# Half the tokens of a product-key expert layer taken from row gathers to dense products over all experts

## What is computed

```
q = (hc @ w_query).reshape(TOKEN_CHUNK, PEER_HEADS, 2, PEER_HALF)
s = einsum('thpd,pkd->thpk', q, sub_keys)
s1, i1 = top_k(s[:, :, 0], 16)
s2, i2 = top_k(s[:, :, 1], 16)
cand = s1[..., :, None] + s2[..., None, :]
top_s, top_c = top_k(cand, 16)
idx = e1 * 128 + e2
g = softmax(top_s)
u = expert_down[idx]
a = gelu(einsum('thkd,td->thk', u, hc))
return einsum('thk,thkd->td', g * a, expert_up[idx])
```

## Time and profile before

| what | value |
|---|---|
| median of three runs | 3043.16 us (3043.06, 3043.16, 3046.47) |
| span of the profiled execution | 3041.3 us |
| PE busy | 2310.2 us |
| DVE busy | 2213.0 us |
| ACT busy | 2033.8 us |
| POOL busy | 1290.5 us |
| moved by DMA | 1152.07 MB, 379 GB/s over the span |
| of it by the gathers' queue | 1075.90 MB |

### The profile page before, as it was taken

The page is one execution under the profiler, slowest core; times in us unless marked ns, Lnnn a source line. Parts: engine busy times, 40 slices in busy tenths (PEclk is TensorE's granted clock), DMA queues, the critical chain, the costliest instruction groups (busy, mean ns, idle before and its releaser), DMA issues.

```text
span 3041.3 us, 38261 instructions
## 1 busy us (share of the span) xinstructions
PE 2310.2 (76%) x13098; PEld 1887.2 (62%) x13098; DVE 2213.0 (73%) x5241; ACT 2033.8 (67%) x3757; POOL 1290.5 (42%) x1164
## 2 busy tenths in 40 slices
PE   8999889888878966777666676677777777666766
PEld 4765577776765656666656566566566666555655
DVE  7897678899965967777776666677776666777744
ACT  4234268898866756776676767766776677666665
POOL 1003144444434644454454444444444444454543
PEclk9999999999989977776677777777677777776766
DMA  6252499999999999999999999999999999999997
GB/s 232 32 209 79 163 382 417 405 401 418 413 415 403 398 419 421 420 421 421 419 419 420 417 415 415 421 415 422 420 408 419 419 417 411 419 417 421 419 421 329
DMA packets 174835, 1152.07 MB, mean 379 GB/s; under 512 B 23472, under 2 KB 25392, under 8 KB 43440
## 3 DMA queue, kind: packets, MB, share of 16 engines
q0 software_dynamic: 147984, 1075.90, 85.7%
q1 hardware_dynamic: 26656, 73.72, 6.6%
HBM read 1142.60 MB, written 5.77 MB: 378 GB/s over the span
## 4 chain that ended last, share of the span: by engine, by line
DMA 37%; DVE 21%; PE 16%; ACT 11%; issue 5%; POOL 1%; POOLq 0%; DVEq 0%; ACTq 0%
DMA pair<-in_experts_dram,idx_g 36%; DVE pair L1942 10%; PE acc_a L1563 5%; ACT pair L1719 5%; PE acc_b L1563 3%; PE pef L1538 2%; ACT w L1717 1%; ACT L1715 1%; PE acc_b L1486 1%; PE turns L1502 1%; POOL pair L1392 1%; ACT L1710 1%; ACT ga L1715 1%; DVE top_i L1870 1%; DVE staged L1871 1%
## 5 line engine op out<-in xcount | busy, mean ns | idle before, releaser
L1392 POOL DMA_INDIRECT pair<-in_experts_dram,idx_g x1024 | 1226.5, 1198 | 1431.3 <-PE acc_a L1563 803.1
L1942 DVE SCALAR_TENSOR_TENSOR pair<-pair,h 128x1024 f32<-128x1024 f32 x1024 | 1247.6, 1221 | 647.3 <-DMA pair<-in_experts_dram,idx_g 645.4
L1719 ACT ACTIVATE pair<-pair,w 128x1024 f32<-128x1024 f32 x1024 | 1176.4, 1149 | 33.3
L1563 PE MATMUL acc_a<-ident,pair 128*128 128x128 f32 x5120 | 853.1, 327 | 364.4 <-ACT pair L1719 361.0
L1563 PEld LDWEIGHTS acc_a<-ident,pair 128*128 128x128 f32 x5120 | 720.4, 170 | 488.7 <-ACT pair L1719 462.3
L1563 PE MATMUL acc_b<-ident,pair 128*128 128x128 f32 x3072 | 595.4, 362 | 288.2 <-ACT pair L1719 287.9
L1563 PEld LDWEIGHTS acc_b<-ident,pair 128*128 128x128 f32 x3072 | 489.9, 188 | 387.2 <-ACT pair L1719 381.6
L1715 ACT ACTIVATE ga<-a 128x1 f32<-128x1 f32 x1024 | 204.4, 200 | 652.5 <-DVE pair L1942 644.2
L1717 ACT ACTIVATE w<-ga,g 128x1 f32<-128x1 f32 x1024 | 301.7, 295 | 33.2
L1538 PE MATMUL pef<-h2t,wq 128*128 128x128 f32 x1536 | 198.7, 293 | 5.9 <-DMA wq<-in_w_query_t_dram 5.9
L1538 PEld LDWEIGHTS pef<-h2t,wq 128*128 128x128 f32 x1536 | 196.8, 211 | 6.2 <-issue 6.2
(11 more groups left out here) (378 smaller groups left out, 2273.3 us busy)
## 6 DMA issues: line engine op xcount, KB each, us to landing
pair<-in_experts_dram,idx_g POOLq DMA_INDIRECT x1024, 13.8
wrow<-in_w_ada_t_dram SPq DMA_DIRECT2D x12, 1024.0 KB, 6.0
pieces<-in_w_query_t_dram SPq DMA_DIRECT2D x18, 512.0 KB, 8.5
wada<-in_w_ada_t_dram SPq DMA_DIRECT2D x16, 512.0 KB, 9.7
wq<-in_w_query_t_dram SPq DMA_DIRECT2D x4, 2048.0 KB, 29.7
out_dram<-h SPq DMA_DIRECT2D x8, 512.0 KB, 8.3
wout_b<-in_w_out_dram SPq DMA_DIRECT2D x1, 4096.0 KB, 33.8
x<-in_x_dram SPq DMA_DIRECT2D x7, 512.0 KB, 12.9
```

Of the source, the lines that this page charges most:

```text
L1392: p.indirect_dma_start(pair[n % R], None, A["experts"], bass.IndirectOffsetOnAxis(ap=idx[:, t % (2 * PH), k:k + 1], axis=0)).then_inc(pair ...
L1563: last = t.matmul(accs[ACC[i]][:, k * P:(k + 1) * P], pair[n % R][:, D + k * P:D + (k + 1) * P], S.ident[:], is_transpose=True, start=n % ...
L1719: s_.activation(pair[n % R][:, D:], pair[n % R][:, D:], ACT.Copy, scale=w[:, n % NA:n % NA + 1]).then_inc(scaled, 1)
L1942: v.scalar_tensor_tensor(down, down, 1.0, h2[:, n // P, :], ALU.mult, ALU.mult, accum_out=a[:, n % NA:n % NA + 1]).then_inc(dotted, 1)
```

## The change

Tiles 0 to 3 keep the gathers, so that `SLOTS` is now 512. Tiles 4 to 7 (512 tokens) are computed over all 16384 experts: first product, gelu, a gate matrix that is zero for the experts a token has not chosen, second product. The experts are taken as 128 chunks of 128, chunk c holding the experts whose second index is c; two new inputs, `down_t` and `up_t`, hold the same weights in that order.

The parts, in the slots' order:

- The tasks 18 to 63 are asked in slots 257 to 302, one per slot, and found in slots 258 to 303, all six parts in one slot. For tiles 4 to 7 the find ends with the two indices and the gates as lists of 128 per token (`lists`) and makes no row index.
- In slots 283, 291, 299 and 307 PE turns a tile's three lists so that tokens lie along the free axis. The masks follow in sixteen slots of eight groups each (284, 285, 288, 289, 292, ... 312, 313). A group is four tokens: DVE makes for each a 128x128 matrix with the weight where the first index fits, and one compare of 128x512 for the second; PE multiplies the two, which gives a token's 128x128 gate matrix; ACT copies it into `w_half`, which holds 64 tokens, scattered with a stride of 256 bytes.
- SP stores `w_half` to DRAM eight times, 4 MB each, in runs of 256 bytes; ACT's next evictions wait for that.
- From slot 314 the 128 chunks run: 8 products of 128x512 into PSUM, gelu on ACT, product with the chunk's gates on DVE (loaded back by SP); and in blocks of four chunks the second product, for each of four tiles 2 x 4 products of 128x512, added into `acc_e` by DVE. These 256 steps are spread evenly over slots 314 to 511. SP loads the weights in pieces of 1 MB, two chunks at a time.
- The gather buffers are eight up to slot 255, three up to slot 315, then five.
- The first phase's semaphores are cleared and freed before the third phase.

The diff, cut to its core (left out are the closing of tiles 4 to 7, `gate_to_row`, the layout of the inputs, and the places in which the engines' loops call the new functions where they only follow the dictionaries):

```diff
-    SLOTS = NT * P
+    OLD = 4
+    SLOTS = OLD * P
+    DT = NT - OLD
+    DENSE_TASK = OLD * PH
...
-    ASKED_AT = [5, 13, 24, 32, 43, 52, 61, 215, 228, 254, 272, 282, 294, 306, 318]
+    ASKED_AT = [5, 13, 24, 32, 43, 52, 61, 215, 228]
+    CLOSE = 2 * PH + 2
+    CLOSE_AT = 257
...
-        if t < 3 * PH:
+        if t < CLOSE:
             return ASKED_AT[t - 9] if t >= 2 * PH else -9
-        return 16 * t - 56
+        return CLOSE_AT + t - CLOSE
...
-        return asked_at(t) + 7
+        return asked_at(t) + 1
...
+    LISTED = {found_at(PH * i + PH - 1) + 4: i for i in range(OLD, NT)}
+    GROUPS_W, HALF_G = P // 4, P // 8
+    MASKED = {}
+    for n, i in LISTED.items():
+        for m, first in ((1, 0), (2, 8), (5, 16), (6, 24)):
+            MASKED[n + m] = [(i - OLD) * GROUPS_W + q for q in range(first, first + 8)]
+    START = max(MASKED) + 1
+    BLOCK, CHUNKS = 4, PK
+    ORDER = []
+    for b in range(CHUNKS // BLOCK + 1):
+        for m in range(BLOCK):
+            if b < CHUNKS // BLOCK:
+                ORDER.append(("first", BLOCK * b + m))
+            if b >= 1:
+                ORDER.append(("second", BLOCK * (b - 1) + m))
+    STEPS, LAST_SLOT = {}, 0
+    for p, step in enumerate(ORDER):
+        LAST_SLOT = START + int(p * (SLOTS - START) / len(ORDER))
+        STEPS.setdefault(LAST_SLOT, []).append(step)
...
+        among = range(R) if n < 2 * P else (6, 7, 1) if n < START + 2 else (6, 7, 1, 2, 3)
...
+            for m in range(2 * DT - 1):
+                sp.wait_ge(w_out, HALF_G * (m + 1))
+                sp.dma_start(w_rows[:, :, m * HALF_T:(m + 1) * HALF_T], w_half[:]).then_inc(w_stored, 16)
...
+                if n == START + 2:
+                    hold(pool, w_done, DT * GROUPS_W)
+                    hold(pool, w_stored, 16 * 2 * DT)
...
+            def masks(m):
+                pe.wait_ge(hot1_ready, 4 * (m + 1))
+                pe.wait_ge(hot2_ready, m + 1)
+                if m >= 2:
+                    pe.wait_ge(w_out, m - 1)
+                for k in range(4):
+                    last = t.matmul(pb[:, (m % 2) * 512 + k * PK:(m % 2) * 512 + (k + 1) * PK], hot1[:, m % 2, k, :], hot2[:, m % 2, k, :],
+                                    start=True, stop=True)
+                last.then_inc(w_done, 1)
...
+            def first_product(c):
...
+                if c >= 2:
+                    pe.wait_ge(gelu_out, c - 1)
+                o = pb[:, (c % 2) * 512:(c % 2) * 512 + 512].rearrange("p (m n) -> p m n", n=P)
+                for k in range(KD):
+                    last = t.matmul(o, down_c[(c // 2) % 2][:, c % 2, k, :], h2[:, OLD:, k * P:(k + 1) * P], start=k == 0, stop=k == KD - 1)
+                last.then_inc(first_done, 1)
+
+            def second_product(step):
+                b, j = step // BLOCK, step % BLOCK
+                if j == 0:
+                    pe.wait_ge(z_ready, BLOCK * (b + 1))
...
+                for n in range(2):
+                    if step >= 1:
+                        pe.wait_ge(added, 2 * step + n - 1)
+                    for c in range(BLOCK * b, BLOCK * b + BLOCK):
+                        last = t.matmul((ob, qs)[n][:], zc[c % 8][:, j * P:(j + 1) * P], up_c[(c // 2) % 4][:, c % 2, n * 512:(n + 1) * 512],
+                                        start=c == BLOCK * b, stop=c == BLOCK * b + BLOCK - 1)
+                    last.then_inc(second_done, 1)
...
+            def masks_out(m):
+                act.wait_ge(w_done, m + 1)
...
+                if m % HALF_G == 0 and m:
+                    act.wait_ge(w_stored, 16 * (m // HALF_G))
+                first = 4 * (m % HALF_G)
+                s_.activation(w_half[:].rearrange("p c t -> p t c")[:, first:first + 4, :],
+                              pb[:, (m % 2) * 512:(m % 2) * 512 + 512].rearrange("p (t c) -> p t c", c=PK), ACT.Copy).then_inc(w_out, 1)
...
+            def dense_gelu(c):
+                act.wait_ge(first_done, c + 1)
+                if c == 0:
+                    act.wait_ge(w_stored, 16 * 2 * DT)
...
+            def make_hot1(m):
...
+                if m >= 2:
+                    dve.wait_ge(w_done, m - 1)
+                for k in range(4):
+                    e1, weight = lists_t[:, i % 2, 0, 4 * q + k:4 * q + k + 1], lists_t[:, i % 2, 2, 4 * q + k:4 * q + k + 1]
+                    v.tensor_scalar(hot1[:, m % 2, k, :], iota_row[:], e1, weight, ALU.is_equal, ALU.mult).then_inc(hot1_ready, 1)
+                v.tensor_tensor(hot2[:, m % 2], bcast(lists_t[:, i % 2, 1, 4 * q:4 * q + 4], 2, [P, 4, PK]),
+                                bcast(iota_row[:], 1, [P, 4, PK]), ALU.is_equal).then_inc(hot2_ready, 1)
...
-            for n in range(SLOTS):
-                if n >= AHEAD:
+            for n in range(LAST_SLOT):
+                if AHEAD <= n < SLOTS:
                     dot(n)
-                if n in FOUND:
-                    find_part(*FOUND[n])
+                for kind, c in STEPS.get(n - 1, ()):
+                    if kind == "first":
+                        mask_product(c)
+                    else:
+                        add_second(c)
...
+                for task, m in FOUND.get(n, ()):
+                    find_part(task, m)
```

More of the change, by code:

```diff
@@ L1574, in turn_back, with turn_lists @@
                 evicted["closed"] = i + 1
+            def turn_lists(i):
+                pe.wait_ge(lists_ready, i - OLD + 1)
+                if i > OLD:
+                    pe.wait_ge(lists_out, i - OLD)
+                for r in range(3):
+                    last = t.transpose(ob[:, r * P:(r + 1) * P], lists[:, i % 2, r, :], S.ident[:])
+                last.then_inc(lists_turned, 1)
+            def masks(m):
[7 more added lines that the diff above has]
+                last.then_inc(w_done, 1)
@@ L1644, in _ @@
                     queries(ASKED[n - 2], (1,))
+                if n in LISTED:
+                    turn_lists(LISTED[n])
+                for m in MASKED.get(n, ()):
+                    masks(m)
+                if n == GATE_ROW_AT:
+                    gate_to_row()
                 if n in SCORED:
@@ L1742, in _ @@
             ready = 1
-            for n in range(SLOTS):
-                if n % TOPK == 0:
+            for n in range(LAST_SLOT):
+                if n < SLOTS and n % TOPK == 0:
                     need = 1 + max(b for b, (first, end) in enumerate(BATCHES) if first <= n // TOPK)
@@ L1748, in _ @@
                         ready = need
-                gelu(n)
+                if n < SLOTS:
+                    gelu(n)
+                for kind, c in STEPS.get(n, ()):
+                    if kind == "first":
+                        dense_gelu(c)
                 if n == AHEAD - 1:
@@ L1907, in find_experts @@
                 own.wait()
+                if task >= DENSE_TASK:
+                    i, h = task // PH, task % PH
+                    if task == DENSE_TASK:
+                        dve.wait_ge(stored, 32)
+                    if h == 0 and i >= OLD + 2:
+                        dve.wait_ge(lists_turned, i - OLD - 1)
+                    own.mark(v.tensor_reduce(lists[:, i % 2, 0:2, h * TOPK:(h + 1) * TOPK], hot[:], AX.X, ALU.add))
+                    return
                 own.step(v.tensor_reduce(key[:], hot[:], AX.X, ALU.add))
@@ new lines, in weigh @@
+                if first >= DENSE_TASK and end % PH == 0:
+                    dve.wait_ge(g_ready, batch + 1)
+                    v.tensor_copy(key[:, 0, :], part_f[:, 0, :]).then_inc(lists_ready, 1)
+            def make_hot1(m):
+                i, q = m // GROUPS_W, m % GROUPS_W
+                if q == 0:
+                    dve.wait_ge(lists_out, i + 1)
+                if m == 0:
+                    dve.wait_ge(iota_made, 2)
+                    dve.wait_ge(up_used, 2 * P)
+                if m >= 2:
[5 more added lines that the diff above has]
+                                bcast(iota_row[:], 1, [P, 4, PK]), ALU.is_equal).then_inc(hot2_ready, 1)
```

244 lines of the change are left out of this document (200 added, 44 removed).

## The result

The changed kernel took **3870.4 us** (median of 4 runs, 3869.8 to 3871.0), the kernel before 3043.1 us beside it (3042.4 to 3046.5). The ratio is 1.272, with a 95% interval of 1.270 to 1.273: slower by 827 us. Forecast were 3942 us and a range of 3790 to 4320.

The account below looks back on a forecast made before the run. The kernel before was taken as DMA-bound by row gathers, 2.53 us a slot. Dense stage starting at 1950 us, 1970 us of it, a 20 us tail and 2 us around the span gave 3942 us; range 3790 to 4320.

Parts of the forecast that it names:

- finds, per slot: Slots 258 to 303: one whole find per slot on DVE, 11.3 us per slot, 520 us in all.
- masks, per group: 128 groups of four tokens: DVE ends last, 1.6 us each with handovers, 205 us in all.
- finds behind masks: In ten of sixteen mask slots the next find waits for last mask, copy, transposes, scores and staging: 30 us.
- four slots without find or mask: Four of slots 304 to 313 run at the pace of three gather buffers, 3.7 us each, 15 us.
- exposed stores: Eight 4 MB mask stores in 256-byte runs hold up the next evictions and the dense gelu: 88 us exposed.
- dense stage: From slot 314: PE packed at clock 1.00, 2048 products at 0.857 us, 198 slots at 0.88, 40 allowed; 1970 us.
- S: Time one 4 MB mask store takes: 35 us with latency, between a floor of 12 and a ceiling of 144.
- toep's copies: Earlier profile's copies to on-chip memory, 4096 runs averaging 288 bytes; gave 32 ns per run for pricing the mask stores.
- Rival 1: Mask stores: short runs cost twice, a store takes 70 us, 368 us exposed, 4220 us in all; chance 0.13.
- The sign of 170 GB/s: Dense stage: DMA moving some 170 GB/s would show the forecast right.
- Rival 2: Dense stage: PE waits each slot for DVE to add both accumulator banks, 515 us more, 4455 us; chance 0.08.
- rival 3: Dense stage: a product costs only 0.22 us, DMA sets the stage, 2857 us in all, faster; chance 0.02.

Follow-up runs that it names:

- longer_finds: Changed kernel with each of the 46 close-stage finds taking the maximum of its 256 sums four times more than needed; 3957.2 us.
- ask_ahead: Changed kernel with a head's queries asked for two slots ahead of its find instead of one in the close stage; 3842.0 us.
- half_k: Changed kernel with the dense stage's first product summing over 4 of its 8 model-dimension blocks, 512 of 4096 products left out; 3439.4 us.
- no_dense_gathers: Changed kernel with row gathers stopped at slot 315, leaving out 196 slots under the dense stage with their transposes and dots; 3695.8 us.
- two_tiles: Changed kernel with only tiles 6 and 7 dense (768 gather slots), a find every fifth slot and a mask group in each slot; 3227.8 us.
- two_half_bytes: two_tiles with the kept gate matrices in bfloat16 instead of fp32, 64 tokens per store buffer; 3229.4 us.

## Why the prediction was right

The direction, the mechanism and the range held; the forecast was 72 us (1.9%) too high. Term by term:

| term | forecast | measured | from |
|---|---|---|---|
| slot 258 begins | 1092 | 1090.9 | its dot |
| finds, per slot | 11.3 | 11.33 | seventeen slots, 266 to 283 |
| masks, per group | 1.6 | 1.63 | TensorE's rows |
| finds behind masks | 30 | 19 | ten waits of 1.86 |
| four slots without find or mask | 15 | 25 | 1.87 + 11.25 + 1.15 + 11.10 |
| exposed stores | 88 | 34 | 27.4 at ScalarE's evictions, 6.5 ahead of the first product |
| close stage in all | 858 | 816 | 1090.9 to 1907.3 |
| dense stage | 1970 | 1945 | 1907.3 to 3851.8 |
| tail | 20 | 16 | to the span's end |

**Up to slot 258** the same slots carried the same work, within 2 us (1092.4 before, 1090.9 after).

**Finds.** Forecast 520 us; measured 46 x 11.33 = 521. The mechanism held, but the hit is luck: two errors cancel. The find itself takes 9.5 us, 1210.88 to 1220.37, and not 9.1, which adds 0.4 us a slot; the wait of every second slot is mostly 0.60 us and not 1.5, which takes nearly 0.45 away. That VectorE's finds lie end to end was shown by longer_finds: 86.8 us for 85 added. That the wait is the scores' was shown by ask_ahead, 28.4 us less. The close stage adds up: 521 for finds, 209 for masks, 34 for stores, 19 in the finds behind masks, 25 in the four slots with neither, and 6 for the first find's wait, which the forecast did not have: 814 of 816 us. In two of the four slots VectorE waits 10 us for a gathered row.

**Masks.** 128 x 1.63 = 209 us against 205. VectorE in order of time, one group:

```profile
1410.73 1.11 DVE L2190 TENSOR_SCALAR hot<-iota_row,lists_t 128x128 f32<-128x128 f32 x4
1411.76 0.68 DVE L2191 TENSOR_TENSOR hot<-lists_t,iota_row 128x512 f32<-128x512 f32 x1
1412.36 1.10 DVE L2190 TENSOR_SCALAR hot<-iota_row,lists_t 128x128 f32<-128x128 f32 x4
```

Four one-hots take 1.03 us from start to start and the compare 0.60, 1.63 in all with no handover between. The forecast had 0.8, 0.66 and 0.14 of handovers: the sum hit by luck, since the one-hots cost more and the handovers nothing. One one-hot was busy 340 ns (142.3 us for 512); such busy times overlap with the next instruction's, as those of the earlier trace rows do, so the group's period, not the sum of its durations (4 x 0.34 + 0.68 = 2.04 us), is the price.

**Stores.** This was the mis-sized term, 54 of the 72 us: S was put at 35 us, and the stores landed in 24.3. The steps behind it (one buffer, the next eviction waits) held: with S = 24 the working's own gaps of 34, 27, 11, 11 and 7 us leave 0 + 0 + 13 + 13 + 17 = 43 us, near the 34 measured. The price per run from toep's copies, 32 ns, was the nearest row but too high; 24.3 us over 1024 runs of each engine are 24 ns with the latency in it.

**Rival 1**, short runs at twice the price, is out: 24 us instead of 70. The Trainium skill, DMA: Bandwidth & Descriptors, section Specifications, says that transfers below 512 B make the DMA engine read, modify and write. By that rule this rival would have been the forecast. The measurement decides: a store of 256-byte runs took 1.75 times one of 32-KB runs (24.3 against 13.9 us), which is a real price, but the 24.3 us are below the 35 that I had taken without the rule. Whether a read stands behind the 1.75 no run here shows.

**Dense stage.** 2048 x 0.857 + 198 x 0.88 = 1930 us leave 15 us for handovers where 40 were allowed. half_k measured 0.842 us a product, no_dense_gathers 0.891 us a slot, so both terms are shown one by one. The sign of 170 GB/s was low: 193 were moved, and TensorE waited for none of it. Rival 2 (lockstep) is out by 0.0 us of idle time ahead of the second products, and rival 3 (a cheap product) by 592 ns a record.

**In short**, where the 827 us come from: after slot 258 the kernel before took some 1949 us at 2.53 us a gather. The change takes away 512 gathers, about 1290 us, and puts 816 us of VectorE's work, mostly bare, 1945 us of TensorE's and 16 us of tail there, 2777 in all and 828 more, under which the 254 gathers that are left cost little: the 58 in the close stage mostly VectorE's dot, the 196 under the dense stage their transposes alone. A dense tile costs 2048 x 0.857 / 4 = 439 us of TensorE, more than the 128 x 2.53 = 324 us of gathers it saves, before a single find or mask is counted.

## What to carry to other kernels

Before an irregular access is replaced by dense arithmetic, price one tile of each on the engine that will bound it: here 439 us against 324 settled the sign, and a kernel with half the dense tiles, whose finds and masks were also spread under the gathers, brought back 643 of 827 us. Price the preparation (here top-k lists and masks) where it will stand, too. In the kernel before, the finds lay under gathers for which VectorE had to wait anyway; where the programs' order puts them nearly alone, they cost their full length; and in two_tiles, where a find came every fifth slot, a slot took 3.95 us (885 for 224) and not a gather's 2.53. Price the waits between engines as well as the work: two_tiles had the work right and missed by 208 us of waits. And a wait that begins at the bound engine's own last instruction is not filled by giving that engine more work; only asking earlier removed it.

## What the runs showed of the hardware that was not expected

- A 128x512 eviction by ScalarE whose elements land far apart took 1.06 us in fp32, at 256 bytes apart (the changed kernel) as at 128 (two_tiles), and 2.48 us in bfloat16 at 128 bytes apart. So the distance did not matter in fp32; whether the bfloat16 eviction is dearer for its element's size or for the conversion no run here separates. A contiguous 128x512 eviction with gelu took 0.60 us.
- Stores by length of run: 4 MB landed in 13.9 us in runs of 32 KB and in 24.3 us in runs of 256 bytes; 2 MB in runs of 128 bytes took 21.7 us (two_tiles) and 26.7 us (two_half_bytes) beside gathers. Reads of 256-byte runs (w_c's 256 KB in 9.2 us) cost the time nothing under TensorE's work.
- DMA engines busy 93 to 95% of a stage did not by themselves hold anybody up: in two_tiles no compute engine waited for a load or a gather from 2000 to 3190 us, at 367 GB/s. TensorE's waits there were almost all for ScalarE.
